# A hybrid diffusion block with 32 experts on one core: the up matrices of the experts are asked for from ScalarE's queue, the second shift is added behind the gather, and the modulation blocks are multiplied as they land

## The chip, the core and the metric

The kernel runs on one core of a Trainium2 chip. The metric is the device time of that core in microseconds (us), as the median of several executions. One further execution was profiled; all rows below are from that one.

## What is computed

256 latent tokens `x` and 256 context tokens `ctx`, each of width 1024, pass one layer. The core of the reference:

```python
mod_x = silu(c) @ w_mod + b_mod                       # 6 x 1024 values; the same for c_ctx
x_sh1, x_sc1, x_g1, x_sh2, x_sc2, x_g2 = split(mod_x, 6)
hx = rmsnorm(x, g_mix) * (1 + x_sc1) + x_sh1          # hc from ctx likewise
ux = hx @ w_in                                        # 512 pool columns, 512 SSM columns
x = x + x_g1 * (concat([pool_mixer(ux_pool), ssm_output(ux_ssm)]) @ w_out)
hx2 = rmsnorm(x, g_ffn) * (1 + x_sc2) + x_sh2
eidx, gate = route(hx2, w_router, b_router)           # best group of 4, then top 2 of its 8 experts
for e in 32 experts, on the tokens routed to e:
    y += gate * ((silu(h @ w_gate[e]) * (h @ w_up[e])) @ w_down[e])
x = x + x_g2 * y
return rmsnorm(x, g_final)
```

`w_gate` and `w_up` are 1024 x 512 per expert, `w_down` is 512 x 1024, all float32: 6 MiB for an expert, 192 MiB for all.

## The kernel before

Each engine's program is written out by hand with semaphores; the order of a queue is the order of its code.

**First part (some 170 us).** `w_mod` comes in 1 MiB blocks of 128 rows and 2048 columns. The first third (r = 0: shift 1, scale 1) is multiplied block by block on TensorE (`mod_chunk(0, k, 4)`, L565). The second third (r = 1: gate 1 and shift 2) is loaded by SyncE's `mod_chunk(k)` (L309) and multiplied by TensorE's `mod_chunk(1, k, 6)` into PSUM bank 6, on top of the bias, which four matmuls put there (L557). The last third (scale 2, gate 2) goes through `last_third` (L314) to VectorE's `mod_sum` (L1486, L1489). Beside it run the SSM (`state_inputs`, `turn_lags`, the HP states on VectorE) and the pool mixer (`u_pool` L683, window L745, `wpool` L752, then ScalarE's scaled copy L1170 into `cat`). The r = 1 row is copied out of PSUM by ScalarE (L1084), written to DRAM (L1167) and read back broadcast over 128 partitions (L347: gate 1 in `g1b` and shift 2 in `sh2b`) and as columns (L348, `sh2c`). VectorE's `rows` (L1530) makes the normalised, scaled and shifted tokens `h2P` for the gather.

**Experts.** Eight rounds of four experts, `four(i)`, i = 0 to 7. A round of TensorE is: `gate_up(i, j)` for the experts 4i+j, j = 0 to 3, in two halves of the contraction, each half counted in `gu_half`; the turns of the hidden values (L951); the scatter of the round before (L908); `down(i)` (L986); and the gather of the next round's tokens by one-hot matrices (L902). `gate_up` works on two buffers `b = j % 2`, each with a gate and an up matrix, filled in halves of 1 MiB:

```python
def gu_load(eng, b, e, half, which="gate up"):        # L246
    ... eng.dma_start(dst[b]... [:, at], src[0, e] ...).then_inc(S(f"gu_in{b}{half}"), 16)
def second_two(i):                                    # L387, SyncE; next_two(i) likewise for 4i+4+b
    for b in range(2):
        for half in range(2):
            sp.wait_ge(S("gu_half"), 8 * i + 2 * b + half + 1)
            gu_load(sp, b, (4 * i + 2 + b) % NE, half)
```

All expert weights are asked for from SyncE's queue, whose loop is `downs(i, 0)`, `second_two(i)`, `downs(i, 1)`, `next_two(i)`; `downs(i, 0)` waits for half of `down` of round i-1 (`down_half`). In round 0, `second_two` and `next_two` are written out in another order (L406 to L417). The last round (i = 7) loads its down matrices in small parts (L432 to L440) and has no `next_two`.

ScalarE, in a round, copies the gathered tokens from PSUM (`take_gathered`, L1217), the results of `gate_up` (`take_gate_up`, L1222), and does Silu (`silu`, L1228). Before round 0 it also copies the two halves of the residual `x2` into the PSUM banks 0 to 3, where the scatter adds (L1211, `outs_started`).

## Time and profile before

| | |
|---|---|
| median of 3 runs (lowest, highest) | 638.4 us (637.27, 638.82) |
| the profiled execution: its time | 638.94 us |
| its span (first to last instruction) | 637.0 us |
| bytes moved by the DMA engines | 246.94 MB, mean 388 GB/s |
| busy: TensorE, VectorE, ScalarE, GpSimd | 91%, 31%, 22%, 8% |

The span is the time from the first instruction to the last; 1.9 us of the execution lie outside it. A busy TensorE is not one at its peak, since matmuls are pipelined. In the rows, PE is TensorE, PEld its weight loads, DVE VectorE, ACT ScalarE, POOL GpSimd, SP SyncE; a q behind it (SPq) is the engine's DMA issuing. `x504` counts instructions. PEclk is the granted TensorE clock as a share of full speed.

### The profile page before, as it was taken

The page shows a single profiled execution, that of the slowest core. Times are in us where ns is not written, and L with a number is a line of the kernel's source. Part 1 is how long each engine was busy: PE and PEld are TensorE (multiplying, and loading weights), DVE is VectorE, ACT ScalarE, POOL GpSimd, SP SyncE. Part 2 cuts the span into 40 slices and gives each one's busy share as a digit, 9 for nine tenths or more (in the row PEclk, how much of TensorE's full clock was granted, in tenths as well). Part 3 has the DMA queues.
Part 4 walks back from the last instruction along what each step waited for, and adds up shares of the span by engine and source line. Part 5 has one row for each costly group of instructions (what it writes and reads, how often), then busy time and mean ns, then how long its engine had stood idle before and what let it go on. Part 6 is the DMA issues. An engine that isn't in the chain of part 4 may idle for free.

```text
span 637.0 us, 9413 instructions
## 1 busy us (share of the span) xinstructions
PE 577.5 (91%) x3798; PEld 244.4 (38%) x3798; DVE 198.2 (31%) x435; ACT 137.2 (22%) x240; POOL 52.6 (8%) x103
## 2 busy tenths in 40 slices
PE   1999999999698997999999899979969997999996
PEld 0455564566442342333334233323423342334331
DVE  7998699969800020010002001000200020010003
ACT  8661351041312120101112020201110111102112
POOL 3895000012000000000000000000000000000001
PEclk9999999999799999999999899989998998999999
DMA  8996387999999899999999999999999999999992
GB/s 330 420 399 265 111 335 269 387 412 419 422 420 421 322 424 422 421 422 389 425 422 422 421 423 422 422 421 423 422 422 421 422 422 422 422 423 417 418 401 82
DMA packets 43498, 246.94 MB, mean 388 GB/s; under 512 B 4664, under 2 KB 7368, under 8 KB 17616
## 3 DMA queue, kind: packets, MB, share of 16 engines
q1 hardware_dynamic: 41960, 243.93, 93.7%
q10 hardware_dynamic: 1160, 1.59, 0.7%
q0 software_dynamic: 352, 1.07, 0.5%
q8 instruction: 18, 0.29, 0.2%
q14 instruction: 8, 0.07, 0.0%
HBM read 244.46 MB, written 2.11 MB: 387 GB/s over the span
## 4 chain that ended last, share of the span: by engine, by line
PE 68%; DMA 23%; DVE 3%; ACT 3%; issue 1%; SPq 1%; POOL 0%; POOLq 0%; DVEq 0%
PE ps L935 24%; DMA wts<-in_w_up 19%; PE ps L986 17%; PE ps L902 5%; DMA wts<-in_w_mod 4%; PE ps L670 4%; PE ps L908 2%; PE ps L683 2%; PE ps L769 2%; PE ps L565 2%; ACT ra L1222 1%; PE ps L703 1%; PE ps L951 1%; PE ps L824 1%; DVE rc L1282 1%
## 5 line engine op out<-in xcount | busy, mean ns | idle before, releaser
L935 PE MATMUL ps<-wts,ra 128*64 128x512 f32 x504 | 234.0, 616 | 25.4 <-DMA wts<-in_w_up 25.4
L936 PE MATMUL ps<-wts,ra 128*64 128x512 f32 x504 | 234.0, 616 | 0.0
L935 PEld LDWEIGHTS ps<-wts,ra 128*64 128x64 f32 x504 | 67.9, 141 | 170.4 <-issue 132.4
L986 PE MATMUL ps<-wts,ra 128*32 128x512 f32 x512 | 111.6, 593 | 0.7 <-DVE ra L1282 0.7
L986 PE MATMUL ps<-rc,ra 128*32 128x512 f32 x512 | 111.6, 593 | 0.0
L1282 DVE TENSOR_TENSOR ra<-ra,ps 128x256 f32<-128x256 f32 x32 | 13.5, 421 | 261.3 <-ACT ra L1228 261.3
L1222 ACT COPY ra<-ps 128x512 f32<-128x512 f32 x32 | 33.5, 1048 | 219.1 <-PE ps L936 219.1
L936 PEld LDWEIGHTS ps<-wts,ra 128*64 128x64 f32 x504 | 67.9, 141 | 0.0
L986 PEld LDWEIGHTS ps<-wts,ra 128*32 128x32 f32 x512 | 29.1, 110 | 74.1 <-issue 73.1
L1282 DVE TENSOR_TENSOR cb<-ps,ra 128x512 f32<-128x512 f32 x32 | 22.1, 692 | 102.7 <-PE ps L986 102.7
L1217 ACT COPY ra<-ps 128x512 f32<-128x512 f32 x32 | 18.8, 586 | 146.2 <-PE ps L902 146.2
L902 PEld LDWEIGHTS ps<-cb,ra 128*128 128x128 f32 x256 | 31.4, 200 | 13.5 <-issue 8.5
L540 POOL TENSOR_SCALAR small<-small 128x1 f32<-128x1 f32 x2 | 0.5, 225 | 431.8 <-ACT ra L1260 431.8
L902 PE MATMUL ps<-cb,ra 128*128 128x128 f32 x256 | 34.5, 291 | 1.0 <-issue 1.0
L670 PE MATMUL ps<-ra,wts 128*128 128x512 f32 x64 | 29.3, 598 | 0.6 <-ACT ra L1105 0.6
L986 PEld LDWEIGHTS ps<-rc,ra 128*32 128x32 f32 x512 | 29.1, 110 | 0.0
L908 PE MATMUL ps<-cb 128*128 128x512 f32 x56 | 26.4, 593 | 0.0
L951 PE MATMUL ps<-cst,ra 128*128 128x128 f32 x128 | 21.0, 287 | 4.4 <-ACT ra L1222 4.4
L951 PEld LDWEIGHTS ps<-cst,ra 128*128 128x128 f32 x128 | 13.4, 140 | 25.8 <-issue 19.5
L565 PE MATMUL ps<-wts,sil 128*32 128x512 f32 x104 | 15.2, 672 | 7.2 <-DMA wts<-in_w_mod 7.2
L1282 DVE TENSOR_TENSOR cb<-cst,ut 128x256 f32<-128x256 f32 x16 | 6.7, 421 | 44.2 <-PE ps L902 42.9
L670 PEld LDWEIGHTS ps<-ra,wts 128*128 128x128 f32 x64 | 11.4, 190 | 13.1 <-issue 11.4
(241 smaller groups left out, 523.5 us busy)
## 6 DMA issues: line engine op xcount, KB each, us to landing
wts<-in_w_up SPq DMA_DIRECT2D x63, 1024.0 KB, 16.7
wts<-in_w_gate SPq DMA_DIRECT2D x63, 1024.0 KB, 15.2
rc<-in_w_down SPq DMA_DIRECT2D x28, 1024.0 KB, 21.1
wts<-in_w_down SPq DMA_DIRECT2D x28, 1024.0 KB, 17.2
wts<-in_w_mod SPq DMA_DIRECT2D x17, 1024.0 KB, 13.8
r<-in_w_mod SPq DMA_DIRECT2D x5, 1024.0 KB, 10.4
wts<-in_w_out SPq DMA_DIRECT2D x2, 2048.0 KB, 11.4
wts<-in_w_down SPq DMA_DIRECT2D x6, 512.0 KB, 16.7
```

Of the source, the lines that this page charges most:

```text
L565: mm = pe.matmul(ps[32 * j:32 * j + 32, bank, :], silc[:, k, :], w[:, 512 * j:512 * j + 512], start=False, stop=(k == KD - 1))
L670: mm = pe.matmul(ps[:, 4 + q % 2, :], WBs[:, k, P * q:P * q + P], hT[:, k, :], start=(k == 0), stop=(k == KD - 1))
L683: mm = pe.matmul(ps[:, t, :], hT[:, k, 256 + P * t:256 + P * t + P], WBp[:, k, :], start=(k == 0), stop=(k == KD - 1))
L902: mm = pe.matmul(o, h2P[:, t, k, :], Pm[:, t], start=True, stop=True, skip_group_check=True)
L908: pe.matmul(ps[:, 2 * t + h, :], PT[:, t, :], oS[:, 2 * h + t, :], start=False, stop=False, skip_group_check=True)
L935: pe.matmul(ps[0:64, 4 + b, :], st, gate_k, start=(k == 0), stop=(k == KD - 1))
L936: mm = pe.matmul(ps[64:128, 4 + b, :], st, up_k, start=(k == 0), stop=(k == KD - 1))
L951: mm = pe.transpose(ps[:, 6 + j % 2, P * f:P * f + P], gu[:, j % 2, P * f:P * f + P], ident)
L986: mm = pe.matmul(ps[32 * j:32 * j + 32, BANKS[n], :], hid[:, j, f, SLOTS * t:SLOTS * t + SLOTS], Wd[j][:, f, 512 * h:512 * h + 512], start ...
L1217: act.copy(xm[:, 2 * r:2 * r + 2], ps[:, GATHER[r], :].rearrange("p (k e s) -> p k e s", k=2, e=4)).then_inc(S("xm_ready"), 1)
L1222: act.copy(gu[:, j % 2, :].rearrange("p (f q) -> p q f", f=FC), ps[:, 4 + j % 2, :].rearrange("p (q f) -> p q f", f=FC)).then_inc(S("gu_co ...
L1282: return dve.tensor_tensor(o, a, b, op)
```

## The change

SyncE's queue keeps the gate and down matrices. From round 1 on, ScalarE asks for the up matrices (both halves at once) after its copy of the `gate_up` that read the old ones. Shift 2 is no longer broadcast to 128 partitions and added in `rows`, but is added per partition, as the bias of ScalarE's copy behind the gather. TensorE's r = 1 blocks 5, 6 and 7 move to where they are expected to have landed; their bias is added by VectorE from a row that is zero elsewhere. Half of the residual is put into PSUM by TensorE (identity matmuls), half by ScalarE as before. The order of SyncE's queue moves with it.

```diff
@@ SyncE
-            sp.dma_start(modrow[0:97:32], b_mod_rows...)   # second DMA
+            sp.wait_ge(S("consts_set"), 3)                 # behind x, ctx and BC
+            sp.dma_start(modrow[0:97:32], b_mod_rows...)
...
-            sp.wait_ge(S("mod_used"), 14)
-            last_third(0, 0)
             sp.wait_ge(S("s_mm"), 8)
             sp.dma_start(wo_pool, w_out_v[:, 0:4, :]).then_inc(S("wo_pool_in"), 16)
-            sp.wait_ge(S("mod_used"), 15)
-            last_third(1, 0)
-            sp.wait_ge(S("mod_used"), 16)
-            last_third(2, 0)
+            for j in range(3):
+                sp.wait_ge(S("mod_used"), 14 + j)
+                last_third(j, 0)
...
             sp.wait_ge(S("pool_mm"), 1)
+            gu_load(sp, 0, 0, 0, "up")
+            sp.wait_ge(S("pool_mm"), 2)
             last_third(3, 0)
-            sp.wait_ge(S("mod1_row"), 16)
-            sp.dma_start(ra[:, 6144:8192], row_dram[0:1].broadcast_to([P, 2048])).then_inc(S("g1_in"), 16)
-            sp.dma_start(sh2c, ...)
-            sp.wait_ge(S("pool_mm"), 2)
-            gu_load(sp, 0, 0, 0, "up")
             for j in range(4):
                 sp.wait_ge(S("mod2_used"), 2 * j + 2)
                 last_third(j, 1)
+                if j == 0:
+                    sp.wait_ge(S("mod1_row"), 16)
+                    sp.dma_start(g1b, row_dram[0:1, 0:D].broadcast_to([P, D])).then_inc(S("g1_in"), 16)
+                    sp.dma_start(sh2c, ...)
...
-                        gu_load(sp, b, (4 * i + 2 + b) % NE, half)           # second_two
+                        gu_load(sp, b, (4 * i + 2 + b) % NE, half, "gate")
...
-                        gu_load(sp, b, (4 * i + 4 + b) % NE, half)           # next_two
+                        gu_load(sp, b, (4 * i + 4 + b) % NE, half, "gate")
@@ TensorE: the r = 1 bias matmuls go; blocks 5, 6, 7 earlier; the Toeplitz products before wpool; and
+            for n in range(2):
+                mm = pe.matmul(ps[:, n, :], ident, x2[:, n // 2, 512 * (n % 2):512 * (n % 2) + 512], start=True, stop=False, ...)
+            mm.then_inc(S("outs_started"), 1)
@@ ScalarE
-            mod_rows(1, 6)
-            act.wait_ge(S("modrow"), 2)
-            act.dma_start(row_dram[0]..., modrow[0:97:32, 1, :]).then_inc(S("mod1_row"), 16)
-            act.wait_ge(S("pool_mm"), 1)
+            act.wait_ge(S("pool_mm"), 2)
             ...                                            # cat <- ps, four activations
+            act.wait_ge(S("modrow"), 2)
+            act.dma_start(row_dram[0]..., modrow[0:97:32, 1, :]).then_inc(S("mod1_row"), 16)
...
-            for t in range(NT):
-                act.copy(ps[:, 2 * t:2 * t + 2, :]..., x2[:, t, :]).then_inc(S("outs_started"), 1)
+            act.copy(ps[:, 2:4, :]..., x2[:, 1, :]).then_inc(S("outs_act"), 1)
...
-                act.copy(xm[:, 2 * r:2 * r + 2], ps[:, GATHER[r], :]...).then_inc(S("xm_ready"), 1)
+                for k in (2 * r, 2 * r + 1):
+                    mm = act.activation(xm[:, k], ps[:, GATHER[r], ...], ACT.Identity, bias=sh2c[:, k:k + 1])
+                mm.then_inc(S("xm_ready"), 1)
...
+            def up_load(i, j):
+                for half in range(2):
+                    act.wait_ge(S("gu_half"), 8 * i + 2 * j + half + 1)
+                    gu_load(act, j % 2, (4 * i + 2 + j) % NE, half, "up")
...
-            def four(i):
+            def four(i, loads=range(4)):                   # four(0, ()), four(i), four(last_four, (0, 1))
                 ...
                 take_gate_up(i, 0)
+                if 0 in loads:
+                    up_load(i, 0)
                 take_gate_up(i, 1)
                 silu(i, 0)
+                if 1 in loads:
+                    up_load(i, 1)
                 ...                                        # 2 after silu(i, 1), 3 after silu(i, 2)
@@ VectorE
+            dve.memset(modrow[:, 1, :], 0.0).then_inc(S("consts_set"), 1)
...
+            dve.wait_ge(S("mod_used"), 2 * KD)             # behind hp_ready, before mod_sum
+            tt(modrow[:, 1, :], modrow[:, 1, :], ps[:, 6, :], ALU.add).then_inc(S("modrow"), 1)
...
-                dve.scalar_tensor_tensor(h2P..., hn[t]..., rstd2[:, t:t + 1], sh2b..., ALU.mult, ALU.add).then_inc(S("h2_rows"), 1)
+                dve.tensor_scalar(h2P..., hn[t]..., rstd2[:, t:t + 1], None, ALU.mult).then_inc(S("h2_rows"), 1)
```

TensorE, from the second `state_inputs` to the pool product (L565: r = 1 blocks; L656: `turn_lags`; L683: `u_pool`; L745: window; L752: `wpool`; L760: Toeplitz). Before:

```order
L703 MATMUL ps<-ra,wts 64x64 x64
L683 MATMUL ps<-wts,ra 128x512 x2
L656 MATMUL ps<-cst,cb 128x128 x8
L683 MATMUL ps<-wts,ra 128x512 x4
L656 MATMUL ps<-cst,cb 128x128 x8
L565 MATMUL ps<-r,sil 32x512 x4
L683 MATMUL ps<-wts,ra 128x512 x2
L565 MATMUL ps<-wts,sil 32x512 x4
L683 MATMUL ps<-wts,ra 128x512 x8
L745 MATMUL ps<-cb 128x128 x8
L565 MATMUL ps<-wts,sil 32x512 x4
L752 MATMUL ps<-cb,lam 128x256 x4
```

TensorE at the same place, changed (L563, L654, L681, L744, L757, L750 in the same roles):

```order
L701 MATMUL ps<-ra,wts 64x64 x64
L563 MATMUL ps<-r,sil 32x512 x4
L654 MATMUL ps<-cst,cb 128x128 x8
L681 MATMUL ps<-wts,ra 128x512 x2
L563 MATMUL ps<-wts,sil 32x512 x4
L681 MATMUL ps<-wts,ra 128x512 x3
L654 MATMUL ps<-cst,cb 128x128 x8
L563 MATMUL ps<-wts,sil 32x512 x4
L681 MATMUL ps<-wts,ra 128x512 x11
L744 MATMUL ps<-cb 128x128 x8
L750 MATMUL ps<-wts,ra 32x128 x32
L757 MATMUL ps<-cb,lam 128x256 x4
```

Block 5 now stands right behind `state_inputs`, block 7 before the last eleven `u_pool` matmuls, and the Toeplitz products before `wpool`.

SyncE at the start of `second_two` in its loop, before:

```order
L263 DMA rc<-in_w_down 128x2048
L391 ISA
L251 DMA wts<-in_w_gate 128x2048
L251 DMA wts<-in_w_up 128x2048
L391 REGISTER_ALU
```

ScalarE in its loop, changed, around the first `up_load` (L1217: gathered tokens; L1224: results of `gate_up`; L1230: Silu):

```order
L1217 ACTIVATE ra<-ps,aux 128x256 x2
L1223 ISA
L1224 COPY ra<-ps 128x128x4
L1236 REGISTER_ALU
L250 ISA
L250 DMA wts<-in_w_up 128x2048
L250 ISA
L250 DMA wts<-in_w_up 128x2048
L1223 REGISTER_ALU
L1224 COPY ra<-ps 128x128x4
L1229 REGISTER_ALU
L1230 ACTIVATE ra<-ps 128x256
```

The up halves left SyncE's queue, where each stood beside its gate half, and stand as a pair behind ScalarE's copy.

## Rows read from the trace of the kernel before

**Rows 1.** Page: GB/s in 40 equal slices of the span

```profile
GB/s 330 420 399 265 111 335 269 387 412 419 422 420 421 322 424 422 421 422 389 425 422 422 421 423 422 422 421 423 422 422 421 422 422 422 422 423 417 418 401 82
```

**Rows 2.** Stretches of 4 us: busy by engine, clock, DMA share, GB/s

```profile
92.00:96.00 4.00, 4.00 (x22) 1.96 (x21) 3.86 (x13) 1.07 (x2) 0.00 (x0) 1.00 0.37 148
...
112.00:116.00 4.00, 4.00 (x66) 2.55 (x55) 3.90 (x8) 1.30 (x4) 0.00 (x0) 1.00 0.92 323
...
168.00:172.00 4.00, 2.34 (x10) 2.21 (x11) 2.87 (x13) 0.10 (x1) 0.00 (x0) 0.52 1.00 418
...
216.00:220.00 4.00, 4.00 (x40) 1.17 (x36) 0.00 (x0) 0.00 (x0) 0.00 (x0) 1.00 0.48 195
220.00:224.00 4.00, 4.00 (x44) 1.22 (x40) 0.00 (x0) 0.00 (x0) 0.00 (x0) 1.00 0.76 250
...
296.00:300.00 4.00, 4.00 (x22) 1.30 (x20) 0.00 (x0) 0.71 (x1) 0.00 (x0) 1.00 0.96 360
```

**Rows 3.** Chain of waits, 76 to 205 us: start, us, what

```profile
76.19 0.99 PE ps L557 x8
...
83.79 3.88 PE ps L703 x128
...
94.77 0.99 PE ps L565 x8
...
158.76 1.13 DVE ra L1530
...
170.75 3.75 PE ps L902 x16
...
178.34 1.98 PE ps L902 x16
...
191.18 13.46 DMA wts<-in_w_up
...
207.41 0.84 PE ps L935
```

**Rows 4.** Timeline, 96 to 206 us: start, us, engine, instruction [idle before]

```profile
96.25 0.47 SPq L335 DMA_DIRECT2D wts<-in_w_out  x1
...
111.73 1.58 ACT L1170 ACTIVATE wts<-ps,vt 128x256 f32<-128x256 f32 x4 [1.55 <-PE ps L752]
...
120.23 0.38 SPq L314 DMA_DIRECT2D r<-in_w_mod  x1
...
168.63 0.66 PE L890 MATMUL ps<-cb,cst 128*128 128x64 f32 x2 [3.45 <-DVE cb L1282]
...
204.69 0.64 PE L935 MATMUL ps<-wts,ra 128*64 128x512 f32 x1 [2.14 <-DMA wts<-in_w_up]
```

**Rows 5.** DMA asked for at 109.59: KB, us to landing

```profile
wts<-in_w_mod SPq DMA_DIRECT2D x1, 1024.0 KB, 5.2
```

**Rows 6.** DMA asked for at 133.06

```profile
rc<-in_w_down SPq DMA_DIRECT2D x1, 1024.0 KB, 17.9
```

**Rows 7.** DMA asked for at 183.95

```profile
wts<-in_w_gate SPq DMA_DIRECT2D x1, 1024.0 KB, 7.0
```

**Rows 8.** DMA asked for by GpSimd at 195.26

```profile
r<-in_g_final POOLq DMA_DIRECT2D x1, 512.0 KB, 8.3
```

**Rows 9.** Timeline around round 2's first `second_two` and the last round's

```profile
290.08 0.33 SPq L251 DMA_DIRECT2D wts<-in_w_gate  x1
290.52 0.38 SPq L251 DMA_DIRECT2D wts<-in_w_up  x1
...
295.66 1.06 ACT L1222 COPY ra<-ps 128x512 f32<-128x512 f32 x1 [3.01 <-PE ps L936]
...
584.77 0.34 SPq L251 DMA_DIRECT2D wts<-in_w_gate  x1
...
605.59 0.64 PE L935 MATMUL ps<-wts,ra 128*64 128x512 f32 x1 [0.40 <-DMA wts<-in_w_up]
```

**Rows 10.** DMA asked for at 342.61, round 3's first `second_two`

```profile
wts<-in_w_gate SPq DMA_DIRECT2D x1, 1024.0 KB, 12.8
```

More of the change, by code:

```diff
@@ L551, in mod_chunk @@
             def mod_chunk(r, k, bank):
[L553 removed]
+                if k == 0 and r == 0:
                     pe.wait_ge(S("bmod_in"), 16)
@@ L747, in _ @@
             mm.then_inc(S("window_mm"), 1)
-            mod_chunk(1, 7, 6)
+            for g in range(8):
+                for q in range(4):
+                    grp = 8 * q + g
+                    mm = pe.matmul(ps[32 * q:32 * q + 32, 4 + g % 2, 128 * (g // 2):128 * (g // 2) + 128], U8[:, g, q, 1, :],
+                                   TT[:, :, SG * grp:SG * grp + SG], start=(g < 2), stop=False, skip_group_check=True)
+            mm.then_inc(S("pool_mm"), 1)
             pe.wait_ge(S("wpool_in"), 16)
@@ L753, in _ @@
                                start=True, stop=True, skip_group_check=True)
-            mm.then_inc(S("pool_mm"), 1)
-            for g in range(8):
-                for q in range(4):
-                    grp = 8 * q + g
-                    mm = pe.matmul(ps[32 * q:32 * q + 32, 4 + g % 2, 128 * (g // 2):128 * (g // 2) + 128], U8[:, g, q, 1, :],
-                                   TT[:, :, SG * grp:SG * grp + SG], start=(g < 2), stop=False, skip_group_check=True)
             mm.then_inc(S("pool_mm"), 1)
@@ L885, in _ @@
             gate_product().then_inc(S("gate_mm"), 1)
+            for n in range(2):
+                mm = pe.matmul(ps[:, n, :], ident, x2[:, n // 2, 512 * (n % 2):512 * (n % 2) + 512], start=True, stop=False,
+                               skip_group_check=True)
+            mm.then_inc(S("outs_started"), 1)
             pe.wait_ge(S("score"), 1)
@@ L1246, in _ @@
                 take_gathered(0, r)
-            four(0)
+            four(0, ())
             for r in range(2):
```

44 lines of the change are left out of this document (24 added, 20 removed).

## The prediction, made before the changed kernel ran

> **What bounds the kernel now.** I read the page first. The GB/s line shows 420 to 425 in nearly every slice from 127 us on, with one dip to 322 (207 to 223 us) and one to 389 (287 to 303), and before that four thin slices, 265, 111, 335 and 269 (48 to 111) [rows 1]. 192 MiB of the traffic are expert weights, so from 127 us on the time is bytes by rate: 1 MiB at 421 GB/s is 2.49 us, and a round of 24 MiB is 59.8. The end can come nearer only by transfer time that now goes idle. Next I read stretches of 4 us to find that idle time. Against 422 GB/s, 92 to 96 us loses 2.6 us and 112 to 116 loses 0.9; these and the four between them, of which 104 to 108 is full, lose 8.9. 216 to 224 loses 2.1 + 1.6 = 3.8, and 296 to 300 loses 0.6 (1.2 with its two neighbours) [rows 2]. Third the chain: up to 178 us it is TensorE and VectorE, from 191 us on it ends in transfers of up matrices, 13.46 us the first, and back in TensorE [rows 3]. Last the times to landing. A 1 MiB transfer that meets an empty queue lands after 5.2 us [rows 5]. What a transfer takes beyond this is the backlog ahead of it, and tells how much earlier the transfers could run before their requests become the limit.
>
> The sum is made against the profiled execution, 638.94 us with a span of 637.0; it lies 0.54 above the median of 638.4, and I subtract the differences from the median.
>
> **Blocks as they land, SyncE's order (term 1).** Block 5 is multiplied at 94.77 [rows 3], so `last_third(0, 0)` and, queued behind it, the 2 MiB of w_out's pool half are asked for at 96.25 at the latest [rows 4]; the queue ran dry at about 93. In the changed order w_out's pool half waits for `s_mm` alone, at the end of the second `state_inputs` (83.79 + 3.88 = 87.7, seven us before block 5's matmul [rows 3]), and three blocks of `last_third` follow at about 88, 92 and 96. The transfers then run through to about 105. They run dry again later: `last_third(0, 1)` is asked for after VectorE's first two sums, at 120.23 now [rows 4], at 120.9 with the new 0.7 us addition ahead of the sums. It meets an empty queue and lands at 126.1. Behind it up to the down half asked for at 133.06 stand 8.5 MiB (gate 1 is now 0.5 MiB, since shift 2 is not broadcast): 126.1 + 8.5 x 2.49 = 147.3. Now it lands at 133.06 + 17.9 = 151.0 [rows 6]. The transfers are 3.7 us ahead there.
>
> How much of this survives is set where the backlog is thinnest: the gate half asked for at 183.95 lands after 7.0 us, so 1.8 above the empty queue's 5.2 [rows 7]. A lead beyond 1.8 us is lost there unless TensorE asks earlier too.
>
> **TensorE's and VectorE's path to 184 us.** Removed: the bias matmuls, 0.99 [rows 3]. Added: block 7 no longer lies in the wait for the window copy, +1.0, so `u_pool` ends when it does now. The Toeplitz products take that wait, but ScalarE's four activations of 1.58 us, hidden by them now, stand between `wpool` and the output product [rows 4]: 1.58 less the 1.0 gained there, +0.6. `rows` loses an operand: 1.13 us now for 512 values [rows 3]. Between nothing and the half of it, I take 0.5 on the path; it gets nearer to nothing if the strided access sets its time. The copies behind the gather become two activations; I take +0.1, since only the first stands alone. The largest piece is the clock. TensorE is idle 3.45 us before 168.63 [rows 4], the granted clock is 0.52 in 168 to 172 [rows 2], the half level of 1.2 GHz, and the first gather takes 3.75 us where the same 16 instructions take 1.98 at full clock, 2.4 GHz [rows 3]. The two identity matmuls (four records in the trace at the usual spacing of 0.43, 1.7 us) stand behind the gate product and fill half of that wait, which costs nothing, as TensorE waits there for the routing. With 1.7 us of idle time left I expect the clock to hold: -1.8. Sum: +0.6 - 0.5 + 0.1 - 1.8 = -1.6. TensorE asks 1.6 us earlier, and of the lead 1.8 + 1.6 = 3.4 remain (3.7 are there). **Term 1: -3.4**; bounds 0 (all of it lost to TensorE's requests) and -5 (the 8.9 us of idle time mostly recovered).
>
> **Round 0 (term 2).** At 202.55 TensorE waits 2.14 us for expert 3's up half [rows 4], and after it matmuls stand 0.84 apart where 0.43 is usual [rows 3]: four spacings at the half clock, 1.7 us. The limit of 1.8 above is also the amount by which TensorE and transfers stood apart: with the lead, that landing comes 3.4 earlier and TensorE 1.6 earlier, so 0.3 us of waiting remain, and the clock holds. `down` then begins earlier against the transfers, the down loads of round 1 wait for its half, and the hole at 216 to 224 us shrinks from 3.8 to 2.1. **Term 2: -1.7**, bounds 0 and -1.7.
>
> **Up matrices from ScalarE (term 3).** What it saves SyncE's queue, some 0.4 us of issuing for each, is under transfers. What it costs is time of request. In round 2 the gate half goes at 290.08 and the up half at 290.52 [rows 9], both into a queue that is all but empty (the hole of 1.2 us around them). In the changed kernel this up half waits for `gate_up(2, 0)` to end and for ScalarE's copy of 1.06 from 295.66 [rows 9], so it goes at 297. In between only one gate half is on its way: 1 MiB, 2.5 us, is not there when the queue wants it. In round 3 the same request lands after 12.8 us, 7.6 above the empty queue's [rows 10], and the delay costs nothing; the later rounds are asked for at the same spacing from a queue that stays full [rows 1]. **Term 3: +2.5**, bounds 0 and +5.0 (2 MiB late).
>
> **Last round (term 4).** With two queues, how is the rate shared? GpSimd's 0.5 MiB, asked for at 195.26 while SyncE's queue had transfers outstanding to 204.6 [rows 3], landed after 8.3 us, at 203.6 [rows 8]: neither last nor at once. If each queue with work gets half, each up half takes 5.0 us. In the last round ScalarE asks for expert 30's up at 585.9 (gate asked for at 584.77, plus the copy), and the four up halves need 2.7 + 4 x 5.0 = 22.6: 608.5. Now the last has landed by 605.59, where TensorE waited only 0.40 [rows 9]. TensorE and ScalarE have nothing to hide 2.9 us, since `down` and the end follow. If ups come first, it costs nothing. I take the middle, **term 4: +1.5**, bounds 0 and +2.9.
>
> The Trainium skill says in "DMA: Bandwidth & Descriptors", section "Queues, rings and completion order", that each DMA engine goes round robin between the queue rows that have work, packet by packet. By that rule alone term 4 would be 2.9; rows 8 agree with sharing, but show no two hardware queues under load.
>
> Sum: -3.4 - 1.7 + 2.5 + 1.5 = -1.1; 638.4 - 1.1 = **637.3 us**. Its own range is 635 to 639.5.
>
> **Rivals.**
>
> *The ups' own lane costs nothing (633.3).* Up matrices pass the down matrices that stand ahead of them in SyncE's queue, TensorE is served sooner in round 1, frees buffers sooner and asks sooner, so the dry place of round 2 closes and the last round's ups come first. Terms 3 and 4 are 0: 638.4 - 5.1 = 633.3. For it: 8 MiB of down halves stand ahead of round 1's loads. Against it: the gates stay behind them, and TensorE needs both. The same result would come from a rate with two queues 1% higher. The Trainium skill's "Rules for kernel authors" on the same page says that spreading transfers over issuing engines doesn't help the bandwidth; no row here shows two such queues for long.
>
> *The first gather stays at half clock, the lead is hidden anyway (639.1).* Two matmuls are not enough to hold the clock, so TensorE asks when it does now, and term 1 is 1.8 - 0.2 = -1.6: 638.4 - 1.6 - 1.7 + 2.5 + 1.5 = 639.1. For it: the clock fell after a wait of 2.14 us too. Against it: two thirds of the wait are filled or gone.
>
> *The ups come late (643.0, slower).* One mechanism: an up half is asked for after the whole `gate_up` and gets half the rate or less. Both deferred halves of round 2 are missed (+5.0), and the last round pays all 2.9. With term 1 at -1.6 and term 2 at -1.7, 638.4 + 4.6 = 643.0. It decides when the up half of expert 4i+3 lands after its gate half. For it: two thirds of the bytes stay in SyncE's queue and keep it busy. Against it: the 7.6 us of backlog in round 3.
>
> **Chances.** A measurement of this kernel tells 0.3%, 1.9 us, from no change. Forecast 0.38, own lane free 0.25, gather at half clock 0.17, late ups 0.20. Of the forecast's range a third lies below 636.5; so faster is 0.25 + 0.12 = 0.37, slower 0.20 + 0.03 = 0.23, and the rest, 0.40, the same. The range of 633.0 to 642.5 takes in the free lane's time and half of the late ups' spread.
>
> **What the changed profile would show.** Term 1: no thin stretch at 92 to 100, one at 116 to 123, and the down half of 133 landing by 148. The path: the first gather's 16 records in 2 us, PEclk 1.00 at 168 to 172. Term 2: no PEclk under 1 at 205 to 209 and the hole behind it near 2 us. Term 3: a hole of about 3.7 us at the start of round 2 with only gate halves outstanding, and none in rounds 3 to 6. Term 4: the last wait for up 31's second half some 2 us, at 607. I am wrong if the GB/s of the full slices moves from 422, or if a wait of more than 1 us for a gate half appears where ups now end the waits.

## The result and the profile after

The changed kernel takes 645.1 us (median of 4 runs, 644.77 to 646.84) against 638.1 for the kernel before on the same chip. The ratio is 1.0114, with a 95% interval from 1.0097 to 1.013: it is slower by 7 us. The forecast of 637.3 is wrong, and so is the range, whose upper end was 642.5. The profiled execution of the changed kernel took 644.77 us, with a span of 642.7; the profiled one of before had 637.0.

The page of the changed kernel, parts 2 and 3 (the slices are 16.07 us each; for a queue: packets, MB, share of the 16 DMA engines' span; q1 is SyncE's queue, q10 ScalarE's):

```profile
span 642.7 us, 9512 instructions
...
PEclk9999999999899998999999897999989999999998
...
GB/s 337 417 400 254 117 406 351 280 417 416 415 400 414 399 423 422 422 381 336 424 422 420 423 423 421 406 424 423 422 422 421 424 421 417 423 422 321 408 377 66
...
q1 hardware_dynamic: 34472, 188.88, 72.8%
q10 hardware_dynamic: 8648, 56.11, 21.0%
```

Against [rows 1] the dip at 207 to 223 us has gone (399 where 322 stood), and two others have come: 381 and 336 (273 to 305, where 422 and 389 stood), and 321 (578 to 594). A full slice is still 420 to 424, so two queues move the bytes at the same rate as one. The 7 in PEclk is 386 to 402 us, a place that comes back below.

Part 5 of the two pages (busy us, mean ns of one, then idle time ahead of the group and what ended most of it) shows where TensorE waits, before and then changed:

```profile
L935 PE MATMUL ps<-wts,ra 128*64 128x512 f32 x504 | 234.0, 616 | 25.4 <-DMA wts<-in_w_up 25.4
...
L986 PE MATMUL ps<-wts,ra 128*32 128x512 f32 x512 | 111.6, 593 | 0.7 <-DVE ra L1282 0.7
```

```profile
L936 PE MATMUL ps<-wts,ra 128*64 128x512 f32 x504 | 230.6, 608 | 18.5 <-DMA wts<-in_w_up 17.1
...
L987 PE MATMUL ps<-wts,ra 128*32 128x512 f32 x512 | 116.5, 611 | 10.1 <-DMA rc<-in_w_down 9.4
```

The wait for up halves fell from 25.4 us to 17.1. The wait of 9.4 us for the second halves of `down` is new; the kernel before has none there.

Stretches of 4 us (columns as in [rows 2]) show the lost transfer time:

```profile
92.00:96.00 4.00, 4.00 (x22) 1.81 (x21) 3.90 (x12) 1.07 (x2) 0.00 (x0) 1.00 1.02 406
...
116.00:120.00 4.00, 4.00 (x11) 1.71 (x9) 3.85 (x6) 0.00 (x0) 0.00 (x0) 1.00 0.46 185
120.00:124.00 4.00, 4.00 (x105) 2.05 (x106) 3.68 (x4) 0.00 (x0) 0.00 (x0) 1.00 0.72 221
...
168.00:172.00 4.00, 2.25 (x14) 2.17 (x15) 3.31 (x14) 0.14 (x1) 0.00 (x0) 0.88 1.02 428
...
216.00:220.00 4.00, 4.00 (x40) 1.17 (x36) 0.08 (x1) 0.00 (x0) 0.00 (x0) 1.00 0.92 320
220.00:224.00 4.00, 4.00 (x38) 2.17 (x31) 3.02 (x5) 0.45 (x2) 0.00 (x0) 1.00 1.01 426
...
284.00:288.00 4.00, 4.00 (x24) 1.84 (x21) 0.00 (x0) 0.13 (x1) 0.00 (x0) 1.00 0.79 324
288.00:292.00 4.00, 3.87 (x23) 1.99 (x23) 0.76 (x2) 1.68 (x4) 0.00 (x0) 1.00 0.74 258
292.00:296.00 4.00, 4.00 (x22) 1.60 (x20) 0.00 (x0) 1.06 (x1) 0.00 (x0) 1.00 0.52 174
...
585.00:589.00 4.00, 4.00 (x21) 1.58 (x19) 0.00 (x0) 1.06 (x1) 0.00 (x0) 1.00 0.34 141
```

I read such stretches, 2 us each, over the whole span, and took as lost what each lies under 422.5 GB/s. Summed, in us:

| stretch | before | after |
|---|---|---|
| 76 to 130 | 13.0 | 11.5 |
| 130 to 204 | 0.5 | 1.9 |
| 204 to 228 (end of round 0) | 3.7 | 0.8 |
| 270 to 325 (start of round 2) | 1.2 | 4.8 |
| 325 to 560 (rounds 2 to 6) | 0.3 | 1.0 |
| 560 to 613 (last round) | 0.6 | 4.4 |

The second ledger is TensorE's: when the first matmul of the next round's gather starts, behind `down`. Round by round it stands -4.3, -3.2, +0.1, +6.9, +3.2, +6.7 and +3.3 us against before (222.43 against 226.71 in round 0, 576.44 against 573.10 in round 6), the last `down` +4.5, the end +5.7. So the changed kernel is 4.3 us ahead after round 0, loses 7.6 by the end of round 6, and 2.4 more in the last round. The zigzag has a pattern in the chain of waits (start, us, what):

```profile
267.40 13.87 PE ps L987 x128
...
301.68 28.32 DMA rc<-in_w_down
330.04 7.07 PE ps L987 x64
...
357.52 34.15 DMA rc<-in_w_down
```

Up to round 1 `down` runs through, 128 matmuls in 13.87 us. From round 2 to round 6 its first half runs, and then TensorE waits for the second halves of the down matrices, which come 28 or 34 us after their request. The waits are 0.3, 4.3, 0.4, 4.2 and 0.3 us: nearly all of the 9.4 us lies in rounds 3 and 5, and a round later half of such a loss is made up again.

### The profile page after: what moved, and what is told of

It is laid out like the page before. It is cut to its first block, busy times and chain, and to the rows that moved or that the text cites. A ratio compares the mean times of both kernels' runs of the same rounds, so it can differ in the third digit from the quotient of the medians.

```text
span 642.7 us, 9512 instructions
## 1 busy us (share of the span) xinstructions
PE 579.4 (90%) x3794; PEld 248.2 (39%) x3794; DVE 198.0 (31%) x437; ACT 143.6 (22%) x270; POOL 52.6 (8%) x103
## 4 chain that ended last, share of the span: by engine, by line
PE 61%; DMA 31%; ACT 2%; SPq 2%; issue 2%; DVE 1%; POOL 0%; ACTq 0%; POOLq 0%; DVEq 0%
DMA rc<-in_w_down 24%; PE ps L936 19%; PE ps L987 13%; DMA wts<-in_w_up 5%; PE ps L903 5%; PE ps L668 4%; PE ps L563 3%; PE ps L766 2%; PE ps L681 2%; PE ps L849 2%; DMA wts<-in_w_mod 2%; PE ps L701 1%; PE ps L587 1%; PE ps L821 1%; PE ps L909 1%
## 5 line engine op out<-in xcount | busy, mean ns | idle before, releaser
L936 PE MATMUL ps<-wts,ra 128*64 128x512 f32 x504 | 230.6, 608 | 18.5 <-DMA wts<-in_w_up 17.1
L937 PE MATMUL ps<-wts,ra 128*64 128x512 f32 x504 | 230.8, 608 | 0.0
L936 PEld LDWEIGHTS ps<-wts,ra 128*64 128x64 f32 x504 | 66.8, 139 | 157.0 <-issue 125.4
L987 PE MATMUL ps<-wts,ra 128*32 128x512 f32 x512 | 116.5, 611 | 10.1 <-DMA rc<-in_w_down 9.4
L987 PE MATMUL ps<-rc,ra 128*32 128x512 f32 x512 | 116.5, 610 | 0.0
L1224 ACT COPY ra<-ps 128x512 f32<-128x512 f32 x32 | 33.5, 1046 | 207.1 <-PE ps L937 207.1
L937 PEld LDWEIGHTS ps<-wts,ra 128*64 128x64 f32 x504 | 66.8, 139 | 0.0
L1217 ACT ACTIVATE ra<-ps,aux 128x256 f32<-128x256 f32 x64 | 26.8, 470 | 155.5 <-PE ps L903 154.6
L766 PE MATMUL ps<-wts 128*128 128x512 f32 (+1 forms) x40 | 15.8, 530 | 1.8 <-ACT wts L1168 1.8
L668 PEld LDWEIGHTS ps<-ra,wts 128*128 128x128 f32 x64 | 11.4, 190 | 13.1 <-issue 11.4
```

The source lines that it names most:

```text
L668: mm = pe.matmul(ps[:, 4 + q % 2, :], WBs[:, k, P * q:P * q + P], hT[:, k, :], start=(k == 0), stop=(k == KD - 1))
L766: mm = pe.matmul(o, cat[:, k, P * (n // 2):P * (n // 2) + P], wo_pool[:, k, c0 + cols.start:c0 + cols.stop], start=(k == 0), stop=False)
L936: pe.matmul(ps[0:64, 4 + b, :], st, gate_k, start=(k == 0), stop=(k == KD - 1))
L937: mm = pe.matmul(ps[64:128, 4 + b, :], st, up_k, start=(k == 0), stop=(k == KD - 1))
L987: mm = pe.matmul(ps[32 * j:32 * j + 32, BANKS[n], :], hid[:, j, f, SLOTS * t:SLOTS * t + SLOTS], Wd[j][:, f, 512 * h:512 * h + 512], start ...
L1217: mm = act.activation(xm[:, k], ps[:, GATHER[r], 256 * (k % 2):256 * (k % 2) + 256].rearrange("p (e s) -> p e s", e=4), ACT.Identity, bias ...
```

## Why the down matrices are late: two kernels, one moment

In round 3 both kernels ask for the last two down halves at the same time, 357.12 us (before) and 357.04 (after). Times to landing, before and then changed (SPq is SyncE's queue; KB each, median us to landing):

```profile
rc<-in_w_down SPq DMA_DIRECT2D x2, 1024.0 KB, 24.2
```

```profile
rc<-in_w_down SPq DMA_DIRECT2D x2, 1024.0 KB, 31.9
```

They are 7.7 us later, 3.1 MiB at 2.49 us. In the kernel before the first of the two lands after 23.2 us, so the last one after 25.2, at 382.7; the second half of `down`, which needs it, begins 6.9 us after the start at 380.25, at 387.1. That is 4.4 us of slack. In the changed kernel the last one lands at 357.52 + 34.15 = 391.7, 9 us later: 4.4 are covered, and nearly all the rest is the wait of 4.26 us that its timeline shows (start, us, engine, instruction, and in brackets idle time and its end):

```profile
391.71 1.07 PE L987 MATMUL ps<-wts,ra 128*32 128x512 f32 x2 [4.26 <-DMA rc<-in_w_down]
391.72 1.07 PE L987 MATMUL ps<-rc,ra 128*32 128x512 f32 x2
392.56 1.07 PE L987 MATMUL ps<-wts,ra 128*32 128x512 f32 x2
```

Behind it the next five spacings are 0.85 us where 0.43 is usual, at the half clock (granted 0.50 from 391.7 to 396.0): 2.1 us on top of the wait.

What passed the down halves is in the queue shares of the changed kernel, for 306 to 310 us:

```profile
q10 hardware_dynamic: 121, 0.86, 51.4%
q1 hardware_dynamic: 118, 0.84, 50.0%
```

While both queues have work, each gets half of the rate (in round 3, at 370 to 374 us, 49.1% and 50.3%). The ups asked for behind the down halves, those of `next_two` for the next round, were behind them in the single queue; from ScalarE's they go beside them. TensorE needs them a round later. The gate half asked for at 363.6 lands after 21.7 us before and after 14.2 in the changed kernel: it comes sooner, while `down` stands.

The Trainium skill says in "DMA: Bandwidth & Descriptors", section "Queues, rings and completion order", that each DMA engine goes round robin between the rows of queues with work, one packet at a time. The trace agrees, 51.4% against 50.0%. Its "Rules for kernel authors" say that spreading transfers over issuing engines doesn't help bandwidth; the trace agrees here too (420 to 424 GB/s in a full slice). What cost the time is the order among them.

## The experiments

Each ratio is to the kernel before on the same chip, with its 95% interval. They ran on several chips, where the kernel before has medians of 637.67 to 638.64, so rows are compared by their ratios. The changed kernel's is 1.0114 (1.0097 to 1.013).

| kernel | median us | ratio (interval) |
|---|---|---|
| all ups back on SyncE | 639.22 | 1.0006 (0.9984 to 1.0028) |
| the same again | 637.56 | 1.0001 (0.9985 to 1.0017) |
| before, with only the queue move | 646.18 | 1.0123 (1.0098 to 1.0148) |
| two queues, ups asked in time | 650.05 | 1.0197 (1.0167 to 1.0226) |
| one queue, ups late | 647.93 | 1.0137 (1.0111 to 1.0163) |
| downs first | 652.36 | 1.0224 (1.019 to 1.0259) |
| first part without the shift | 637.17 | 0.9992 (0.9977 to 1.0006) |
| gates early | 638.97 | 1.0013 (0.9994 to 1.0031) |
| last round's ups back | 644.20 | 1.0093 (1.0071 to 1.0115) |
| ups of rounds 1 and 2 back | 643.82 | 1.0085 (1.0056 to 1.0113) |
| ScalarE asks in rounds 3 to 6 only | 641.93 | 1.0069 (1.0043 to 1.0095) |
| ScalarE asks in `next_two` only | 645.23 | 1.0112 (1.0092 to 1.0133) |
| ScalarE asks in `second_two` only | 645.07 | 1.0105 (1.0083 to 1.0128) |

### The queue move undone, and done alone

The changed kernel with all ups on SyncE's queue beside their gates:

```diff
-                        gu_load(sp, b, (4 * i + 2 + b) % NE, half, "gate")     # next_two likewise
+                        gu_load(sp, b, (4 * i + 2 + b) % NE, half)
...
-            def four(i, loads=range(4)):
+            def four(i, loads=()):
```

> The changed kernel with one part undone: all up matrices go back to SyncE's queue, beside their gate halves; blocks, order of the first part, shift behind the gather stay. Idle transfer time that the changed kernel has beyond the old one after 240 us is 8.7 us (3.6 at the start of round 2, 0.7 in rounds 3 to 6, 4.4 in the last round). If the queue move is the whole loss, this run gives 645.1 - 8.7 = 636.4 us, below the 638.1 of before by the 3.1 us less of idle time before 240 us less what is given back. If the first part's edits cost something of their own, it is at or above 638.

The kernel before with `up_load` on ScalarE and nothing else:

```diff
-                        gu_load(sp, b, (4 * i + 2 + b) % NE, half)             # next_two likewise
+                        gu_load(sp, b, (4 * i + 2 + b) % NE, half, "gate")
...
+                if 0 in loads:
+                    up_load(i, 0)                                             # and 1, 2, 3, as in the change
```

> The old kernel with one part of the change alone: from round 1 on ScalarE asks for the up matrices, behind its copy, SyncE for gate and down. If the queue move is the whole loss and adds to the rest: 638.1 + 8.7 = 646.8 us, with a hole at the start of round 2 and of the last round. If the loss came from the two together (an earlier first part that leaves the loop a thinner backlog), it is 640 to 642.

The queue move alone costs 1.23%, some 7.9 us. All the rest of the change together makes no difference that these runs can tell (1.0006 here, and 1.0001 when run again below, with intervals from 0.9984 to 1.0028); the 636.4 expected of it didn't come. In TensorE's ledger the second kernel loses 7.2 us against before from round 0 to the end of round 6, and its span is 7.3 longer. Its profile has the same wait, 10.3 us at L986 where the changed kernel has 9.4:

```profile
L986 PE MATMUL ps<-wts,ra 128*32 128x512 f32 x512 | 117.1, 613 | 11.0 <-DMA rc<-in_w_down 10.3
```

ScalarE's issuing isn't what holds TensorE up: in the rounds TensorE waits 3.8 us for ScalarE's copies in the kernel before and in the changed one.

### Late requests or a shared rate?

My first two theories were that the ups are asked for too late (A), or that the down halves wait for their share of the rate (B). Two kernels keep one of the two each. In the first ScalarE asks for each up half as soon as its half of the buffer is free, ahead of its copy:

```diff
-            def up_load(i, j):
-                for half in range(2):
-                    act.wait_ge(S("gu_half"), 8 * i + 2 * j + half + 1)
-                    gu_load(act, j % 2, (4 * i + 2 + j) % NE, half, "up")
+            def up_half(i, j, half):
+                act.wait_ge(S("gu_half"), 8 * i + 2 * j + half + 1)
+                gu_load(act, j % 2, (4 * i + 2 + j) % NE, half, "up")
...
-                take_gate_up(i, 1)
-                silu(i, 0)
-                if 1 in loads:
-                    up_load(i, 1)
+                if 1 in loads:
+                    up_half(i, 1, 0)
+                    up_half(i, 1, 1)
+                take_gate_up(i, 1)
+                silu(i, 0)
```

> The changed kernel, two queues as there, but ScalarE asks for each up half as soon as its own half of gate_up is counted, ahead of its copy: at the moment at which SyncE asks for the gate half. Theory A (late requests: the halves asked for 3.4 to 7 us later leave the queues dry at the start of round 2 and of the last round): the holes close, 636 to 638 us. Theory B (the two queues share the rate by halves, ups pass down matrices, and TensorE waits in down for a down half that landed late): the request's moment does not matter much, 643 to 645 us, and TensorE still waits on rc<-in_w_down.

In the second everything is on SyncE's queue, and both up halves are asked for behind the second gate half:

```diff
                         gu_load(sp, b, (4 * i + 2 + b) % NE, half, "gate")      # next_two likewise
+                    for half in range(2):
+                        gu_load(sp, b, (4 * i + 2 + b) % NE, half, "up")
```

> The changed kernel with one queue (all on SyncE's), but the up halves asked for late: both after the second half of their gate_up. Theory A (late requests): the holes stay, 642 to 645 us. Theory B (shared rate): with one queue nothing passes the down halves, no wait on rc<-in_w_down, 636 to 638 us.

Neither is faster than the changed kernel, and the first is clearly slower. Each theory missed both times, for one kernel even the direction: A said that the first would be as fast as before, B the second. In the first the dry places didn't close but grew, from 4.8 to 6.5 us at the start of round 2 and from 4.4 to 6.0 in the last round. It isn't a clean test of sharing, since its copies stand behind ScalarE's issuing, and TensorE waits 7.6 us for them in all, where the changed kernel has 4.4. But part 5 of the two pages shows that each kind of wait is there without the other. First asked in time (down waits, 17.9 us), then one queue (ups waits, 30.3 us, and no wait for down):

```profile
L936 PE MATMUL ps<-wts,ra 128*64 128x512 f32 x504 | 225.3, 599 | 12.1 <-DMA wts<-in_w_up 10.7
...
L987 PE MATMUL ps<-wts,ra 128*32 128x512 f32 x512 | 121.9, 633 | 18.7 <-DMA rc<-in_w_down 17.9
```

```profile
L940 PE MATMUL ps<-wts,ra 128*64 128x512 f32 x504 | 236.5, 624 | 31.7 <-DMA wts<-in_w_up 30.3
...
L991 PE MATMUL ps<-wts,ra 128*32 128x512 f32 x512 | 111.6, 593 | 0.7 <-DVE ra L1302 0.7
```

### The down halves ahead of the gates

If only the wait for the down halves counted, asking for them sooner would cure it. SyncE's loop in the changed kernel:

```diff
                 downs(i, 0)
+                downs(i, 1)
                 second_two(i)
-                downs(i, 1)
                 next_two(i)
```

> The changed kernel (two queues, ups asked for late), with one edit in SyncE's loop: the second halves of the down matrices are asked for ahead of the gate halves of second_two instead of behind them. Theory B (shared rate; the down halves behind the gates land 28 to 34 us after their request and TensorE waits 9.4 us for them in the rounds): the waits on rc<-in_w_down in down are gone and the 4 MiB fill the hole at the start of round 2, so 638 to 641 us. If those waits only stand where another wait would (the order of two equally needed things), TensorE waits the same time for gate halves and the run stays at 644 to 647 us. The last round has its own order and keeps its hole of 4 us in both.

652.36 us, the slowest of all, far above both times expected. The wait for down is gone, and the wait for ups is 33.7 us. The gates are not asked for late: in round 3 the first goes 0.04 us after the gather at 351.47, and so it does in the changed kernel (342.83 after 342.79).

```profile
351.51 0.33 SPq L250 DMA_DIRECT2D wts<-in_w_gate  x1
```

What has changed is that 4 MiB of down halves, asked for from 346.00 on, stand ahead of gates that TensorE needs before them. That this order makes the wait for ups longer is argued, not shown by a run of its own. TensorE comes to the last round's gather 8.1 us later than in the changed kernel (590.26 against 582.12), and until then the queues have next to nothing to fetch. Stretches there:

```profile
580.00:584.00 4.00, 4.00 (x44) 1.17 (x36) 1.59 (x3) 0.00 (x0) 0.00 (x0) 1.00 0.64 227
584.00:588.00 4.00, 3.96 (x32) 2.40 (x26) 1.93 (x4) 1.68 (x4) 0.00 (x0) 1.00 0.00 0
588.00:592.00 4.00, 4.00 (x28) 2.33 (x24) 0.00 (x0) 0.61 (x2) 0.00 (x0) 1.00 0.18 33
```

No byte moves for 4 us, and 560 to 613 us loses 13.1 us where the changed kernel loses 4.4. Asking for something sooner is no gain when it goes ahead of what is needed first.

### Where the first part's gain stays

Three kernels without the queue move ask what the rest is worth. The first is the kernel before with the new order of blocks, bias and SyncE's first part, but without the shift behind the gather and the identity matmuls (its edits against the changed kernel with the ups back):

```diff
-            pe.matmul(ps[:, n, :], ident, x2...)                              # x2 copied by ScalarE alone, as before
-                    mm = act.activation(xm[:, k], ..., ACT.Identity, bias=sh2c[:, k:k + 1])
+                act.copy(xm[:, 2 * r:2 * r + 2], ...)                        # shift 2 added in rows again
```

> The old kernel with the blocks and the order of the first part alone: all loads on SyncE's queue, shift 2 broadcast and added in rows as before, both residual copies by ScalarE. The kernel with the ups back differs from it by the shift and the identity matmuls. If the lead of the transfers (2.4 us at 183 us in the changed kernel) comes from the blocks, this has the lead less 1.2 us for the wider broadcast, and 637 to 638.5 us; if the blocks give nothing, 638.5 to 640.

The second is the changed kernel with the ups back, once more, beside it:

> The kernel with the ups back on SyncE's queue again, for the size of its difference: 1.0006 with an interval of 0.9984 to 1.0028 the first time. Its trace has the transfers 2 us ahead at 183 us, but the clock fell at 203 us as before. If the lead reaches the end it is 0.3% below before; if the thin backlog in round 0 and the clock eat it, within 0.2%.

The third asks for expert 1's gate halves sooner, since the thin place of the backlog is near 183 us:

```diff
             last_third(3, 0)
+            sp.wait_ge(S("hp_ready"), 1)
+            for half in range(2):
+                gu_load(sp, 1, 1, half, "gate")
...
-            sp.wait_ge(S("hp_ready"), 1)                                      # behind last_third(3, 1)
-            for half in range(2):
-                gu_load(sp, 1, 1, half, "gate")
```

> The kernel with the ups back, and the two gate halves of expert 1 asked for when hp_ready has come (118 us), ahead of last_third(0, 1), not behind y_mm (131 us). They fill the hole of 5.8 us that all changed kernels have at 112 to 124 us. If idle transfer time anywhere in the first part shortens the whole, this gains up to 2 MiB, 5 us: 633 to 635 us. If the thin place at 183 us decides (there the backlog of the kernel with the ups back is 1.6 us), it gains at most 1.6 us: 636 to 638 us, and the gate half asked for at 183 lands 5.2 us after its request, the time of an empty queue.

0.9992, 1.0001 and 1.0013: none differs from the kernel before by what these runs can tell, and the 633 to 635 us that the third was to reach if every idle stretch counted are out. The ledger of the third says that time was moved, not won: 76 to 130 us loses 9.3 instead of 11.2, 130 to 204 loses 3.5 instead of 1.4.

The kernel with the ups back was profiled twice, on two chips, and its spans are 636.2 and 633.0 us. The whole difference lies in round 0. Stretches of the first profile and of the second:

```profile
204.00:208.00 4.00, 4.00 (x14) 1.02 (x10) 0.00 (x0) 0.00 (x0) 0.00 (x0) 0.66 1.01 428
...
216.00:220.00 4.00, 4.00 (x44) 1.19 (x39) 0.00 (x0) 0.00 (x0) 0.00 (x0) 1.00 0.40 117
```

```profile
204.00:208.00 4.00, 2.75 (x16) 1.20 (x12) 0.84 (x2) 1.90 (x4) 0.00 (x0) 1.00 1.01 426
...
216.00:220.00 4.00, 4.00 (x40) 1.17 (x36) 0.56 (x1) 0.00 (x0) 0.00 (x0) 1.00 0.94 340
```

Where the clock falls, near 203 us, `down` starts at 211.1 instead of 208.0, and 204 to 228 us loses 4.2 us instead of 1.2. The same instructions give either. What the two profiles have gained by then stays nearly whole: at the gather behind round 0 the two are 1.6 and 4.8 us ahead of before, at the end 0.8 and 4.0. But the second is the fastest of its twelve runs. The twelve of each spread over 635 to 641 us, and 3 us of that can be this fall; a gain of 1 to 2 us doesn't show in such a median.

### Which rounds?

By the ledger the loss sits at the start of round 2 and in the last round. Three kernels take ScalarE's requests back there. Last round:

```diff
-            second_two(last_four)                                             # SyncE
+            second_two(last_four, "gate up")
...
-            four(last_four, (0, 1))                                           # ScalarE
+            four(last_four, ())
```

> The changed kernel, but the two ups of the last round are asked for from SyncE's queue beside their gates again. In the changed kernel the last round (560 to 613 us) loses 4.4 us of transfer time, 0.6 in the kernel before: 3.8 us. Theory P (the loss lies where the transfer time is idle, and is made by that round's own late requests): 645.1 - 3.8 = 641.3 us. Theory Q (the idle time is only where a lag of all rounds comes out, since every round's last piece comes late): the hole stays or moves ahead, 644 to 646 us.

Rounds 1 and 2, with round 2 written out ahead of the loops on SyncE and ScalarE:

```diff
-            second_two(1)
-            next_two(1)
+            second_two(1, "gate up")
+            next_two(1, "gate up")
+            downs(2, 0)
+            second_two(2, "gate up")
+            downs(2, 1)
+            next_two(2, "gate up")
...
-            with act.Fori(1, last_four) as i:                                 # four(1, ()) and four(2, ()) ahead of it
+            with act.Fori(3, last_four) as i:
```

> The changed kernel, but the ups asked for in rounds 1 and 2 go from SyncE's queue beside their gates again; from round 3 on ScalarE asks, with the last round. The start of round 2 (270 to 325 us) loses 4.8 us of transfer time in the changed kernel, 1.2 in the kernel before. Theory P: the 3.6 us come back, 645.1 - 3.6 = 641.5 us. Theory Q: the first round with ScalarE's requests has the hole instead (near 350 us), 644 to 646 us.

And both edits at once:

> Both at once: ScalarE asks for the ups in rounds 3 to 6 alone. My prediction said that there, with a full queue, late requests cost nothing. Theory P: like the kernel without the queue move, 638.4 us (637 to 640), a loss of 0.7 us at most. Theory Q: one hole remains, at the first round with ScalarE's requests, 641 to 643 us.

The medians came down by 0.9 us (644.20), 1.3 (643.82) and 3.2 (641.93), where 3.8, 3.6 and 7.4 us more of transfer time were lost than in the kernel before; only the third is clear of the changed kernel by the intervals. That isn't because lost transfer time costs nothing. In each of the fifteen profiles the span, less what the ledger from 76 to 613 us has lost, is 616.5 to 618.5 us, while the spans run from 633.0 to 650.5. But a loss taken out of one place comes back in another. The first and the third edit left 2.3 and 2.2 us lost in the last round, where the kernel before has 0.6, and in the first's profile the clock fell near 203 us, so that 204 to 228 us loses 4.0 where the changed kernel's profile loses 0.8. ScalarE's requests in rounds 3 to 6 alone, with a full queue, cost 0.69%, some 4 us. Theory Q's times are met by the first and third and missed by 0.2 us by the second, theory P's by none. But Q's place for the third was wrong: there is no hole at the first round with ScalarE's requests (325 to 560 us loses 1.0 us). In the chain of that kernel the late down halves begin in exactly that round:

```profile
319.61 13.87 PE ps L991 x128
...
353.88 35.22 DMA rc<-in_w_down
```

This profile is of one of its fastest runs (639.4; the twelve lie between 639.0 and 646.7), and I have none of a slow one. In it TensorE waits 10.6 us for down halves, and the span is 0.6 above before: such a wait costs little as long as the transfers go on.

### The two kinds of up load, one at a time

That left open whether rounds 3 to 6 lose by late requests or by down halves that are overtaken. The ups of `second_two` are wanted in the same round; those of `next_two` are asked for behind the down halves and wanted last. First ScalarE asks for `next_two`'s alone, then for `second_two`'s alone:

```diff
-                        gu_load(sp, b, (4 * i + 2 + b) % NE, half, "gate")
+                        gu_load(sp, b, (4 * i + 2 + b) % NE, half)
...
-            def four(i, loads=range(4)):
+            def four(i, loads=(2, 3)):
```

```diff
-                        gu_load(sp, b, (4 * i + 4 + b) % NE, half, "gate")
+                        gu_load(sp, b, (4 * i + 4 + b) % NE, half)
...
-            def four(i, loads=range(4)):
+            def four(i, loads=(0, 1)):
```

> The changed kernel, but the ups of second_two (experts 2 and 3 of a round) are asked for by SyncE beside their gates again; ScalarE asks for those of next_two (the next round's experts 0 and 1) alone. These are asked for with over 20 us of backlog, and are needed last of all that is outstanding. Overtaking theory: they get half the rate while the down halves asked for before them wait in SyncE's queue, so down halves land 31 us and more after their request in round 3, TensorE waits for rc<-in_w_down in every second round, and the time is 642 to 645 us. Lateness theory (the loss comes from up halves asked for too late for their own use): nothing here is asked for late, 637 to 639.5 us, no wait for down. The dry places at the start of round 2 and in the last round should be gone or small (under 1.5 us lost in each).

> The other half: ScalarE asks for the ups of second_two alone, next_two's are with their gates on SyncE's queue. Overtaking theory: at most 2 MiB of ups stand beside the down halves, so these land at most 2.5 us later than before and TensorE waits little for them (under 5 us in all); what is left is the late request: holes at the start of round 2 and in the last round of about 4 us each as in the changed kernel, 640 to 643 us. Lateness theory: the whole loss is here, 643 to 646 us.

The mechanisms come apart. TensorE's two longest waits from 228 us on (us in total, times, longest), `next_two` alone and then `second_two` alone:

```profile
PE ps L987 <- DMA rc<-in_w_down: 19.4, 5, 4.9
PE ps L936 <- DMA wts<-in_w_up: 7.7, 5, 2.7
```

```profile
PE ps L936 <- DMA wts<-in_w_up: 26.8, 10, 7.4
PE ps L952 <- ACT ra L1224: 3.8, 7, 0.6
```

And the last two down halves of round 3, in the same order, where the kernel before has 24.2:

```profile
rc<-in_w_down SPq DMA_DIRECT2D x2, 1024.0 KB, 30.9
```

```profile
rc<-in_w_down SPq DMA_DIRECT2D x2, 1024.0 KB, 24.3
```

With `next_two` alone the ups that ScalarE asks for are wanted last, and TensorE waits for down halves in every round from 2 to 6, not in every second one: this half of the move costs 1.12% by itself, just past the upper end of what the overtaking theory gave. These ups too are asked for later than before, and no run has the overtaking without that; but TensorE waits for ups less (7.7 us) than in the kernel before (23.3). The lateness theory, 637 to 639.5 here, is out. The waits for down become lost transfer time in the last round: TensorE reaches it late, its second gate half is asked for at 590.69 where the kernel before has 584.77, and the queues run dry meanwhile. With `second_two` alone TensorE waits for no down half; the ups are late, the start of round 2 loses 4.3 us and the last round 3.1: lateness costs 1.05% by itself, more than the overtaking theory left for it (643 us at most; 645.07). My dry places were wrong for the first of the two kernels (2.7 and 6.2 us lost, where I had said under 1.5). Both costs are real, and the changed kernel, which has both, is no slower than either alone by these medians.

## Why the prediction was wrong, by its own steps

Two steps failed. The cost of the queue move, terms 3 and 4, was put at +4.0; it is 7.9 (1.0123) where it is the only change. The gain of the first part, terms 1 and 2, was put at -5.1; where it is the only change the medians show none (1.0006 and 1.0001). With either of the two right the sum would have been 641.2 or 642.4, just in the range.

**Terms 1 and 2, -3.4 and -1.7: near their sum in one profile, by luck, and nothing in the medians.** In the profile of the changed kernel `down` of round 0 starts 4.3 us sooner (208.49 against 212.76), 5.1 were forecast. The transfers run through at 92 us (406 GB/s) and thin out at 116 to 124, as said. The down half asked for at 133.35 lands at 148.35, 2.7 us ahead of before where 3.7 were forecast. But at the thin place TensorE's request goes at 183.38, only 0.6 us sooner than before (183.95), not 1.6. The gate half then lands as into an empty queue:

```profile
wts<-in_w_gate SPq DMA_DIRECT2D x1, 1024.0 KB, 5.2
```

So by the prediction's own rule 1.8 + 0.6 = 2.4 us of the lead remain and not 3.4. The missing 1.0 us is in TensorE's path. Its wait was 1.72 us, as forecast, but the gather took 3.15 us and not 2, since the clock fell all the same (0.88 in 168 to 172). The changed kernel's timeline there:

```profile
168.72 0.41 PE L891 MATMUL ps<-cb,cst 128*128 128x64 f32 x2 [1.72 <-DVE cb L1298]
...
170.38 3.15 PE L903 MATMUL ps<-cb,ra 128*128 128x128 f32 x16 [1.03 <-issue]
```

Term 2 made up for it: the clock held at 204 to 208 (1.00), and the hole behind shrank to 0.8 us, better than the 2.1 forecast. That was the luck. Of the 13 profiles taken of kernels with the new first part (two of them with another edit in it), 204 to 228 us loses 4.0 to 4.7 us in 7 and 0.8 to 1.9 in 6 (3.7 in the kernel before). Term 2 is a state that some executions reach, and I priced it as certain.

**Term 3, +2.5 (bounds 0 and +5.0): the step whose mechanism failed.** By TensorE's ledger it measured +7.6 up to the end of round 6 (7.2 with the queue move alone): 4.4 by the end of round 2, and 3.2 more in rounds 3 to 6, where I wrote that "the delay costs nothing". At the start of round 2 only the size was off. Behind the first gate half the queue has one request where it had two:

```profile
286.99 0.33 SPq L250 DMA_DIRECT2D wts<-in_w_gate  x1
...
292.88 0.33 SPq L250 DMA_DIRECT2D wts<-in_w_gate  x1
...
293.00 0.85 ACTq L250 DMA_DIRECT2D wts<-in_w_up  x2
```

From 287 to 293 us 1 MiB is on order and not the 2 MiB of [rows 9]; the stretch from 270 to 325 loses 4.8 us, 3.6 more than before, where I had 2.5. The error of mechanism is in rounds 3 to 6. I asked of them only whether an up half comes in time, and found 7.6 us of backlog. I did not ask what the up halves do to the transfers ahead of them. I had the sharing by halves in hand, for term 4, and used it only in the last round. With it the last down half of round 3 is 9 us later and had 4.4 us to give.

**Term 4, +1.5 (0 to +2.9): measured +2.4 by TensorE's ledger, in its bounds, but by another way; lost transfer time rose by 3.8.** I foresaw slow up halves and no hole. The up halves went right behind the second gate half, as forecast (1.1 us behind, 584.77 and 585.9):

```profile
588.05 0.33 SPq L250 DMA_DIRECT2D wts<-in_w_gate  x1
...
588.17 0.84 ACTq L250 DMA_DIRECT2D wts<-in_w_up  x2
```

What I left out is the first up half, which used to go beside the first gate half (582.34 here). For 5.8 us one MiB was on order where there had been two, and a dry place of 4.4 us was the result, the same as in round 2. It had been foreseen there and not here. At 597 to 601 us the two queues share the rate by halves (51.5% and 50.0%), as the upper bound had it.

**The rivals.** The late ups (643.0, chance 0.20) were nearest and on the right side, but name only half: the second mechanism, ups that pass the down halves, was in none of them. The free lane (633.3) saw the overtaking and took it for a gain: up matrices "pass the down matrices that stand ahead of them". They do, and it is the down matrices that TensorE needs next. I was to be wrong if full slices moved from 422 GB/s or a gate half made TensorE wait; neither happened, and the list lacked the down halves.

**What stays open.** Why the two costs don't add (1.12% and 1.05% alone, 1.14% together). In part it may be the clock near 203 us, which held in the changed kernel's profile and fell in the other two (0.8 us lost behind it against 4.0 and 4.5); past 228 us the three lose 8.2, 7.2 and 5.7 us of transfer time more than before. Open too is what makes the clock fall there in one execution and hold in another, and why rounds 3 to 6 alone spread over 8 us. That the lead of the first part reaches the end is seen in two profiles and shown by no median.

## What to carry to other kernels

A queue is also an order. Before a stream is split over two queues, list the outstanding transfers in the order in which they are needed, and ask of each one whether something needed later now shares its rate; a backlog protects the transfer that joins it, and not the ones that it passes. For a kernel bound by its transfers read both ledgers, lost transfer time and the start of the same instruction round by round: here the first pointed at two places, and the edits for both gave back 3.2 us in the median of the 7.4 lost there. And don't book a gain that hangs on the clock holding behind a wait until several executions show it.

## What the runs showed of the hardware

- Two hardware queues with work share the rate by halves (51.4% and 50.0% at 306 to 310 us, 50.3% and 49.1% at 370 to 374), and together move no more than one: 420 to 424 GB/s in a full slice with either.
- One wait of TensorE, 4.26 us, is followed by five spacings of 0.85 instead of 0.43 us, at the half clock (granted 0.50): half as much again as the wait itself.
- The same kernel, profiled on two chips, had spans of 636.2 and 633.0 us, by a fall of the clock in 204 to 208 us (0.66 against 1.00) that the transfers turned into a hole.
